# Cache compression: a cached request's pages through the first MLP layer as three rounded products per position pair, its pages issued from SP, GpSimd and ScalarE

## The reference

```python
def compress(kv, pe, w1, w2):
    b, t = kv.shape[:2]
    r = CMP_BLOCK // CMP_STRIDE
    n_c = (t - CMP_BLOCK) // CMP_STRIDE + 1
    pieces = kv[:, :(n_c + r - 1) * CMP_STRIDE].reshape(b, n_c + r - 1, CMP_STRIDE, NSA_KV_HEADS, HEAD_DIM)
    pe_r = pe.reshape(r, CMP_STRIDE, HEAD_DIM)
    w1_r = w1.reshape(r, CMP_STRIDE, HEAD_DIM, CMP_HID)
    hid = sum(jnp.einsum('bncgd,cdf->bngf', pieces[:, p:p + n_c] + pe_r[p][:, None, :], w1_r[p]) for p in range(r))
    return jnp.einsum('bngf,fd->bngd', jax.nn.gelu(hid), w2)
```

## Time and profile before

| | us |
|---|---|
| median of 3 runs | 4158.97 (4150.61 to 4160.83) |
| span of the profiled execution | 4159.6 |
| setup, to the barrier's end on TensorE | 0 to 84 |
| cache stage on TensorE | 84 to 1307 |
| TensorE busy in the whole span | 3572.3 |

### The profile page before, as it was taken

One profiled execution on the slowest core, in us unless ns is written; L12 is line 12 of the kernel. 1 busy time (PEld: TensorE's weight loads), 2 busy tenths in 40 slices (PEclk: granted clock), 3 DMA queues, 4 the chain that ended last, 5 costly groups with the idle time before them and its releaser, 6 DMA issues. The chain is left out here.

```text
span 4159.6 us, 51003 instructions
## 1 busy us (share of the span) xinstructions
PE 3572.3 (86%) x16964; PEld 2681.6 (64%) x16964; DVE 1200.2 (29%) x2981; ACT 721.6 (17%) x1413; POOL 459.6 (11%) x692
## 2 busy tenths in 40 slices
PE   2899999999998796469699994578998779999997
PEld 1555555555555455355477772258887679999996
DVE  0111111111112104610155552112112344444445
ACT  0211111111111101200143340002111221111112
POOL 3222231322200000000000002720000000000000
PEclk9999999999999896669688876558999889999998
DMA  8455464545513100040300001313112212111111
GB/s 138 75 96 95 88 92 84 94 90 89 94 46 125 62 0 0 18 157 0 128 11 11 10 0 59 105 42 97 46 40 71 92 61 61 35 56 35 55 30 41
DMA packets 311388, 263.21 MB, mean 63 GB/s; under 512 B 45835, under 2 KB 282879, under 8 KB 310313
## 3 DMA queue, kind: packets, MB, share of 16 engines
q1 hardware_dynamic: 204184, 166.18, 15.5%
q0 software_dynamic: 31232, 50.90, 6.1%
q10 hardware_dynamic: 75792, 44.27, 5.1%
HBM read 232.71 MB, written 32.48 MB: 64 GB/s over the span
## 5 line engine op out<-in xcount | busy, mean ns | idle before, releaser
L354 PE MATMUL bank<-xt,cw 128*128 128x511 f32 x2048 | 892.4, 594 | 2.4 <-ACT xt L412 2.0
L354 PEld LDWEIGHTS bank<-xt,cw 128*128 128x128 f32 x2048 | 385.4, 191 | 469.4 <-issue 468.5
L412 DVE COPY xt<-bank 64x512 f32<-64x512 f32 x256 | 176.1, 688 | 937.5 <-PE bank L346 933.6
L168 POOL DMA_DIRECT2D raw<-in_cache_nsa_kv x512 | 310.3, 606 | 827.2 <-issue 827.2
L1909 PE MATMUL bank<-u2H,fwiH 128*128 128x344 f32 x1056 | 338.3, 320 | 38.2 <-DVE fwiL L2285 38.2
L1909 PE MATMUL bank<-u2H,fwiL 128*128 128x344 f32 x1056 | 337.9, 320 | 0.0
L1909 PE MATMUL bank<-u2L,fwiH 128*128 128x344 f32 x1056 | 337.8, 320 | 0.0
L1909 PEld LDWEIGHTS bank<-u2H,fwiH 128*128 128x128 f32 x1056 | 199.5, 189 | 38.7 <-issue 38.7
L1909 PEld LDWEIGHTS bank<-u2H,fwiL 128*128 128x128 f32 x1056 | 199.2, 189 | 0.0
L1909 PEld LDWEIGHTS bank<-u2L,fwiH 128*128 128x128 f32 x1056 | 198.9, 188 | 0.0
L412 ACT ACTIVATE xt<-bank 64x512 f32<-64x512 f32 x256 | 151.3, 591 | 160.4 <-PE bank L346 157.3
(11 more groups left out here) (436 smaller groups left out, 5063.1 us busy)
## 6 DMA issues: line engine op xcount, KB each, us to landing
raw<-in_cache_nsa_kv POOLq DMA_DIRECT2D x512, 64.0 KB, 4.8
raw<-in_cache_nsa_kv SPq DMA_DIRECT2D x512, 64.0 KB
wada<-in_w_ada ACTq DMA_DIRECT2D x48, 512.0 KB, 6.2
fwi<-in_w_ffn_in SPq DMA_DIRECT2D x44, 512.0 KB, 4.1
fwo<-in_w_ffn_out SPq DMA_DIRECT2D x22, 512.0 KB
gwg<-in_w_in SPq DMA_DIRECT2D x20, 512.0 KB, 3.9
wada<-in_w_ada_final ACTq DMA_DIRECT2D x16, 512.0 KB, 4.3
mw<-in_w_in SPq DMA_DIRECT2D x3, 2048.0 KB, 10.0
```

Source lines behind the costliest of these rows:

```text
L168: eng.dma_start(k.raw[8 * q:8 * q + 8, kv, nt], pages[bass.ds(at, 1), :, :, P * kv:P * kv + P] .rearrange("o n s c -> (o n) s c")).then_in ...
L354: mm = pe.matmul(k.bank[4 + c][:, 0:NCMP], w1[:, kv, j // 8, j % 8, P * c:P * c + P], xt[:, kv, g, j % 8, j // 8:j // 8 + NCMP], start=(j ...
L412: ins = eng.activation(dst, src, ACT.Copy) if odd else eng.tensor_copy(dst, src)
```

## The change

`setup` and `cache_compress` become one stage, `cache_stage`, without a barrier between them, and without loops: all 16 items are written out. The items come kind by kind: 8 items of keys, then 8 of values.

The first layer: a tile Q is one item's pair q of neighbouring token positions (8 tiles per item, 128 in all). Its four accumulators, banks 0 to 3, live over the item's 8 tiles. Each gets 2 `mm3` per tile, 24 matmuls of 512 columns in all. The transposes of pair Q+2 run between the accumulators of tile Q, in banks 4 and 5. ScalarE copies each transpose out rounded (`xH`, two activations of 64x512), and VectorE subtracts that from PSUM and keeps the rest (`xL`); a ring of 4 pairs holds them. The weights are rounded and split once for each kind, on the same engines.

The modulation: instead of 128 columns of weights as the stationary operand and 9 moving columns, the conditioning vectors, padded to 32 columns, are stationary, and the weights move, 512 columns at a time, into four groups of 32 PSUM partitions. 32 steps of 4 such fp32 matmuls, one after every third tile. Its weights come in 1 MB pieces.

The pages: of an item's 64 pages SP issues 24, GpSimd 24 and ScalarE 16. ScalarE issues those of the first two items before anything else it computes, and those of a later item in four lots of 4, behind the tiles with q = 7, 0, 1 and 2. The loads of small tensors move from SP to ScalarE's queue. The table of biases holds 1152 entries instead of 8320, and the attention's index into it is clamped to match.

The core of the diff:

```diff
-NREV = 8320
+NREV = 1152
+REV0 = PAST + P - NREV
...
+def load_page(k, eng, t, page, sem):
+    kv, b = t // B, t % B
-    at = eng.value_load(k.pt[0:1, bass.ds(i * NPAGES + page, 1)], min_val=0, max_val=POOL - 1)
+    at = eng.value_load(k.pt[0:1, b * NPAGES + page:b * NPAGES + page + 1], min_val=0, max_val=POOL - 1)
+    eng.dma_start(k.raw[8 * q:8 * q + 8, t % 2, nt], pages[bass.ds(at, 1), :, :, P * kv:P * kv + P]
+                  .rearrange("o n s c -> (o n) s c")).then_inc(sem, 16)
...
+    NITEM = 2 * B
+    NQ = 8 * NITEM
+    RING = 4
...
+    steps = [(2 + 3 * n if n < 16 else 64 + 4 + 3 * (n - 16), n // DK, n % DK) for n in range(4 * DK)]
+    STEP = {at: (r, kk) for at, r, kk in steps}
+    TURN = {at + 1: r for at, r, kk in steps if kk == DK - 1}
+    PEBV = 57
+    chunks = [("w1", 0, 0), ("w1", 0, 1)] + [("ada", r, kk) for r in range(2) for kk in range(DK)] \
+        + [("w1", 1, 0), ("w1", 1, 1)] + [("ada", r, kk) for r in (2, 3) for kk in range(DK)]
+    at_chunk = {x: n for n, x in enumerate(chunks)}
...
+        def pages(eng, first, count, sems):
+            for t in range(NITEM):
+                if t >= 2:
+                    eng.wait_ge(s_tr, 16 * (t - 1))
+                load_pages(k, eng, t, first, count, sems)
...
+            sp.wait_ge(k.s_pt, 16)
+            pages(sp, 0, 24, k.s_page_sp)
...
+            pages(pool, 24, 24, k.s_page_pool)
...
+            def turn(f):
+                t, s = f // 16, f % 16
+                if s == 0:
+                    pe.wait_ge(k.s_page_sp[t % 2], 16 * 24 * (t // 2 + 1))
+                    pe.wait_ge(k.s_page_pool[t % 2], 16 * 24 * (t // 2 + 1))
+                    pe.wait_ge(k.s_page_act[t % 2], 16 * 16 * (t // 2 + 1))
+                if f >= 2:
+                    pe.wait_ge(s_xl, 2 * f - 2)
+                for nt in range(4):
+                    mm = pe.transpose(k.bank[4 + f % 2][:, P * nt:P * nt + P], raw[:, t % 2, nt, s, :], k.ident[:, :])
+                mm.then_inc(s_tr, 1)
...
+            def modulation(r, kk):
+                n = at_chunk["ada", r, kk]
+                pe.wait_ge(s_stg[n % 2], 16 * (n // 2 + 1))
+                if kk == 0 and r:
+                    pe.wait_ge(s_mod, r)
+                for j in range(4):
+                    mm = pe.matmul(k.bank[7][32 * j:32 * j + 32, :], cT[:, kk, :], stg[:, n % 2, 512 * j:512 * j + 512],
+                                   start=(kk == 0), stop=(kk == DK - 1))
+                mm.then_inc(s_ada, 1)
...
+            def tile(Q):
+                t, q = Q // 8, Q % 8
+                if t % B == 0:
+                    pe.wait_ge(s_wL, 8 * (t // B) + q + 1)
+                pe.wait_ge(s_xl, 4 * Q + 4)
+                for n in range(4):
+                    c, g = n // 2, n % 2
+                    if q == 0 and t:
+                        pe.wait_ge(s_gelu, 4 * t - 3 + n)
+                    for r in range(2):
+                        x = slice(r, r + NPIECE)
+                        mm = mm3(pe, k.bank[n][:, :], (wH[:, q, r, P * c:P * c + P], wL[:, q, r, P * c:P * c + P]),
+                                 (xH[:, Q % RING, g, x], xL[:, Q % RING, g, x]), q == 0 and r == 0, q == 7 and r == 1)
+                    if q == 7:
+                        mm.then_inc(s_hid, 1)
+                    if n % 2 == 0 and Q + 2 < NQ:
+                        turn(2 * (Q + 2) + n // 2)
+                    if q == 1 and n == 1 and t:
+                        second(t - 1)
+                    if q != 7 and n == 3:
+                        mm.then_inc(s_xq, 1)
...
+            bias(0)
+            for f in range(4):
+                turn(f)
+            pe.wait_ge(s_w2, 32)
+            for Q in range(NQ):
+                tile(Q)
+                if Q == PEBV:
+                    for j in range(2):
+                        n = at_chunk["w1", 1, j]
+                        pe.wait_ge(s_stg[n % 2], 16 * (n // 2 + 1))
+                    pe.wait_ge(s_mod, 2)
+                    bias(1)
+                if Q in TURN:
+                    turn_modulation(TURN[Q])
+                if Q in STEP:
+                    modulation(*STEP[Q])
+            second(NITEM - 1)
...
+            stage(act, 0)
+            stage(act, 1)
+            act.dma_start(perow[:, :], k.i["cmp_pe"][0].rearrange("v (j s) d -> (v j) (s d)", s=2)).then_inc(s_pe, 16)
...
+            act.wait_ge(k.s_pt, 16)
+            for t in range(2):
+                load_pages(k, act, t, 48, 16, k.s_page_act)
...
+            def round_weights(kv, q):
+                act.activation(wH[:, q], weights_of(q), ACT.Copy).then_inc(s_wH, 1)
+            def copy(f):
+                Q, s2 = f // 2, f % 2
+                act.wait_ge(s_tr, f + 1)
+                if Q >= RING:
+                    tile_used(Q - RING)
+                for g in range(G):
+                    act.activation(xH[HD * s2:HD * s2 + HD, Q % RING, g, 0:NPIECE], k.bank[4 + f % 2][HD * g:HD * g + HD, :], ACT.Copy).then_inc(s_xh, 1)
...
+            for q in range(8):
+                round_weights(0, q)
+            for f in range(4):
+                copy(f)
+            act.wait_ge(s_wL, 8)
+            act.wait_ge(s_pebs, 1)
+            stage(act, 2)
+            stage(act, 3)
+            act.wait_ge(s_mz, 3)
+            for Q in range(NQ):
+                t, q = Q // 8, Q % 8
+                for s2 in range(2):
+                    if Q + 2 < NQ:
+                        copy(2 * (Q + 2) + s2)
+                    if q == 7:
+                        gelu(t, 2 * s2)
...
+                if Q - 1 in STEP:
+                    n = at_chunk[("ada",) + STEP[Q - 1]]
+                    if n + 2 < len(chunks):
+                        act.wait_ge(s_ada, len([x for x in chunks[:n + 1] if x[0] == "ada"]))
+                        stage(act, n + 2)
+                if q == 3 and t:
+                    store(t - 1)
+                u, part = (Q - 7) // 8 + 2, (Q - 7) % 8
+                if Q >= 7 and part < 4 and u < NITEM:
+                    act.wait_ge(s_tr, 16 * (u - 1))
+                    load_pages(k, act, u, 48 + 4 * part, 4, k.s_page_act)
...
+            def rest(f):
+                Q, s2 = f // 2, f % 2
+                for g in range(G):
+                    dve.wait_ge(s_xh, 2 * f + g + 1)
+                    x = slice(HD * s2, HD * s2 + HD)
+                    dve.tensor_tensor(xL[x, Q % RING, g, 0:NPIECE], k.bank[4 + f % 2][HD * g:HD * g + HD, :], xH[x, Q % RING, g, 0:NPIECE], ALU.subtract).then_inc(s_xl, 1)
...
-            dve.tensor_scalar(bidx[:, :], k.bank[5][0:64, 0:TOPN], hrow[:, :], None, ALU.add).then_inc(s_bidx, 1)
+            dve.tensor_scalar(bidx[:, :], k.bank[5][0:64, 0:TOPN], float(REV0 // SEL), hrow[:, :], ALU.max, ALU.add).then_inc(s_bidx, 1)
...
-            setup(k)
-            k.stage_done()
-            cache_compress(k)
+            cache_stage(k)
             k.stage_done()
```

More of the change, by code:

```diff
@@ L332, in _ @@
                                        peT[:, 16 * kv + j:16 * kv + j + 1], start=(j == 0), stop=(j == 15))
-            mm.then_inc(s_peT, 1)
-            pe.wait_ge(s_peb, 1)
-            def turn(i, kv, tokens, start=False):
-                for s in tokens:
-                    if s == 0:
-                        for nt in range(4):
-                            pe.wait_ge(s_page[kv][nt], i * 256 + 256)
-                    if not (start and s < 4):
-                        pe.wait_ge(s_xta if s % 2 else s_xtv, i * 16 + (8 * kv + s // 2 - 1))
-                    for nt in range(4):
-                        mm = pe.transpose(k.bank[s % 4][:, P * nt:P * nt + P], raw[:, kv, nt, s, :], k.ident[:, :])
-                    mm.then_inc(s_tr, 1)
@@ L374, in modulation @@
-            def modulation(i, kv, n):
-                pe.wait_ge(k.s_ada[n], i * 32 + (16 * kv + 16))
-                if n == 0:
-                    pe.wait_ge(s_modT, i * 2 + (kv + 1))
-                for c in range(DK):
-                    mm = pe.matmul(k.bank[6][:, 9 * n:9 * n + 9], k.wada[:, n, c, :], k.cT[:, c, :], start=(c == 0), stop=(c == DK - 1))
-                if n == 3:
-                    mm.then_inc(s_mod, 1)
-            def item(i, kv, following):
-                pe.wait_ge(s_xtv, i * 16 + (8 * kv + 8))
-                pe.wait_ge(s_xta, i * 16 + (8 * kv + 8))
-                for n in range(4):
-                    first(i, kv, n)
-                    modulation(i, kv, n)
-                    if n == 2:
-                        second(i, kv, 0)
-                    if following:
-                        turn(*following, range(4 * n, 4 * n + 4))
-                second(i, kv, 1)
@@ L396, in _ @@
-            turn(0, 0, range(STRIDE), True)
-            with pe.Fori(0, B - 1) as i:
-                item(i, 0, (i, 1))
-                item(i, 1, (i + 1, 0))
-            item(B - 1, 0, (B - 1, 1))
-            item(B - 1, 1, None)
-        def copy(eng, i, kv, s, first=False):
-            odd = s % 2
-            if s < 2 and not first:
```

(32 more changed lines are left out.)

379 lines of the change are left out of this document (180 added, 199 removed).

## The result

The changed kernel took **4030.5 us** (median of four runs, 4007.5 to 4033.0), beside 4159.9 us for the kernel before (4150.6 to 4162.4): a ratio of 0.968, 95% interval 0.965 to 0.971. It is faster by 129 us. The prediction was 4012 us with a range of 3915 to 4130. A second set of four runs of the same kernel, taken later, gave 4019.1 us (4006.9 to 4023.8).

What follows compares the result with a forecast made beforehand. TensorE's own work was taken to bound the cache stage. Start 100, TensorE 1013 and ScalarE's excess 44 us, plus some 3, gave 1160 against 1307, so 4012 us; range 3915 to 4130 for 8 in 10.

Steps and rivals of the forecast that it cites:

- The tile: First layer on TensorE: 24 products at 0.227 us and 8 transposes at 0.132 us, 6.5 us per tile.
- The modulation: Modulation on TensorE in the loop: 32 steps x 4 matmuls x 2 passes, one after another, 111.5 us.
- the first rival: Modulation's four groups run side by side: 111.5 us becomes 27.9, 37 back for lost cover, time 3965; chance 0.28.
- A page on ScalarE: ScalarE's issue of one page, load plus 742 ns DMA: 1.64 to 2.05 us, taken as 1.84.
- the slower rival: ScalarE's queue fills during bursts: page 3.16 us, time 4305; decides from 2.49 us; page over 2.1 us, chance 0.14.
- What stands ahead of the pages: ScalarE's four copies in a burst tile: 1.8 us of them stand before the first page.
- The cover: TensorE's work in four burst tiles, 33.5 us, against ScalarE's 36.6: excess 3.1 us in 14 items, 44 us.
- the prediction's sign: TensorE idle before L310 or the products in tiles q = 0 to 3, not 5 to 7, some 3 us per item.
- The clock: TensorE's clock in the waits: a fall costed at nothing, since TensorE is ahead there.
- The start: Before the first product: ScalarE's loads 22 us, 32 pages 59 to 75, some 10 more; taken as 100 us.
- What hides at nothing: Page issue in the loop: SP's 49 us per item plus 4.8 to land, and POOL's 32, cost nothing.
- Behind the stage: After the cache stage: only two small operations change, costed at nothing.

Runs made afterwards that it cites:

- The spread kernel: Changed kernel with ScalarE's same 16 pages spread two or three behind each of seven tiles instead of four lots of 4: 3909.3 us, ratio 0.941.
- the half split: Changed kernel with SyncE issuing 32 of an item's 64 pages, GpSimd 32 and ScalarE none: 4018.2 us, ratio 0.966.

## Why the prediction was right, and where it was not

The time missed by 18 us (0.5%), in the predicted direction and range. The end of the cache stage was foreseen at 1160 us and came at 1165. But that agreement is made of errors that cancel:

- **The tile: right.** 24 products at 227 ns and 8 transposes make 6.5 us. In the trace a tile that waits for nothing takes 6.46 us from start to start. The products alone start 233 ns apart at the median, inside the bounds; the transposes cost a little less than taken. Times 128: 827 us, against 828.
- **The modulation: wrong.** The sum let the four matmuls run one after another, 111.5 us. They run side by side: a step 1.07 us, 34.1 us in all, 77 less. This was the first rival, with 0.28. The Trainium skill, TensorEngine Tiling (Array Packing), "Key Properties", says that separate tiles can multiply in parallel, and this trace agrees (eight passes in 1.07 us; 0.55 us each where they stand apart, 139.5 / 256). The rival's time, 3965 us, did not come all the same. Its waits, some 81 us by its sum, came at 84; but it too put the clock at nothing, which cost 41, and the start and the part behind the stage where they were, which cost 10 and 13 more.
- **The second layer: 11 us too long.** It was kept at 63.6 and took 52.8 (L324 and L326). L324 writes halves in turn, eight passes in 1.94 us, and shows the same overlap in pairs.
- **A page on ScalarE: the load right, the DMA wrong.** By the prediction "its DMA should cost the 742" of SyncE's: it costs 1183. The load, 548, lies between the two taken. A page comes every 2.23 us (median between issues inside the loop's lots of four), above the bound of 2.05 and below the 2.49 from which the slower rival decides. The prediction gave a page over 2.1 us 0.14, and put all of it level with now or slower; by its own 22 us for each 0.1 us that begins only near 2.4, and 2.23 would be 4099. The Trainium skill's floor for a load, in DMA: Bandwidth & Descriptors, "Latency and other measured facts", about 600 ns, is none here: ScalarE's median is 548 and its least 445, GpSimd's median 285.
- **What stands ahead of the pages: wrong, the other way.** Of the copies 1.8 us were to come before the first page. In the trace lots of four pages follow one another by 9.37 us at the median (42 pairs of lots), 4 x 2.23 + 0.4: the issues run under the copies. So ScalarE's time for four tiles was 37.5 us where 36.6 had been foreseen, from two errors.
- **The cover: wrong.** TensorE's work in these four tiles was to be 33.5 us. It is 4 x 6.46 + 1.1 for a step + 1.9 to 3.6 for the second layer, some 29 to 31, since the modulation and the second layer are shorter. So the excess isn't 3.1 us per item but some 7 to 9; 83.8 us of waiting in the loop, 6.0 in each of 14 items, is what shows of it. By the starts in the trace the waits lie in the tiles with q = 1 to 4 and in no others, one tile later than the prediction's sign had them: the chain from pages to copies to transposes was right, its length was not.
- **The clock: wrong.** It was put at nothing "since TensorE is ahead there": it is not ahead there, it has just waited. The spread kernel shows 41 us less busy time for the same matmuls (30 against the second trace). The prediction had named a clock that falls in the waits as a sign of being wrong, and it fell.
- In sum: 827 us of tiles, 34 of modulation, 53 of second layer and 11 of bias (L296, 11.4) are 925, not 1013; waits and clock are 84 + 41 = 125, not 44. That makes 1050 where the loop has 1054.8; the 5 left I can't assign. So the 1057 of the prediction held 88 us too much in one part and 81 too little in the other. That these met is luck.
- **The start: 10 us late**, 110.5 instead of 100. That ScalarE begins its pages at 22 us and needs some 10 after them was right (22.6; 10.6). 32 pages took 77.3 us, 2.41 each, where 59 to 75 stood.
- **What hides at nothing: right for after.** No wait on pages but the first shows in the loop. It was right with little to spare: the half split shows what SyncE costs with 32, and the kernels with shorter loops wait for pages now and then.
- **Behind the stage: 13 us more than foreseen**, 2865.3 us of the span after the last second layer against 2852.5 before. The attention stage took 20 more, and other stages gave 7 back. The prediction took this part as unchanged.

So of the 18 us by which the span misses the sum (4030.6 against 4012.6), 5 are the cache stage's end, and 13 lie behind it, where a stage that the change doesn't touch ran at a lower granted clock. In the second trace of the kernel the same two parts are 7 us less and 9 more than foreseen (the stage ends at 1153.4 us, 2861.5 follow), so the miss is of the size by which two executions differ.

## What to carry to other kernels

The cost of moving DMA issues to a busy engine is its own issue time, and what counts is where it stands: the same 16 pages cost the loop 110 to 119 us in lots of four in front of the copies and almost nothing two or three to a tile. A wait on the engine that bounds a stage costs more than its length, since the clock is lower behind it; and a cover is only as long as the work in it, so an estimate of some work that is too long hides a stall as well. When a sum agrees with the result, compare its terms too: here 81 us too little for the waits and the clock hid behind 88 too much for TensorE's work.

## What the runs showed of the hardware

- One 64 KB page costs each issuing engine differently: the DMA instruction 594 ns on GpSimd, 756 on SyncE, 1183 on ScalarE, and from issue to issue 1.24, 2.11 and 2.23 us at the medians. GpSimd was the cheapest.
- Four fp32 matmuls with 32 stationary columns each, one directly behind another and into separate groups of partitions, ran side by side: eight passes in 1.07 us, against 1.05 us for the two passes of one with other products between the four.
- Behind a wait of 2.15 us products started 0.43 us apart instead of 0.23, at a granted clock of 0.50 instead of 1.00, and over the loop the lower clock came to 41 us in one trace and 30 in another.
- An unchanged stage with the same work took between 464 and 490 us in different traces, at a granted clock of 0.78 to 0.74.
